# Retention queries decayed by VectorE before the last attention norm, row scalings on ScalarE, and roots as power steps on GpSimd, in a two-block kernel

## What is computed

```python
# attention, per head
w = p[:, :, 0] - lam * p[:, :, 1]
oa = _rms(w @ v, subln_w) * (1.0 - lambda_init)
# retention, per head and direction (chunks of 128, g = decay of the head)
dmat = where(mask, exp(log_g * max(n - m, 0)), 0)
xi   = exp(log_g * (n + 1));  zeta = exp(log_g * (127 - n))
inner = ((q @ k.T) * dmat) @ v
cross = (q * xi) @ state
state = exp(log_g * 128) * state + (k * zeta).T @ v
orr = _rms(forward + backward)              # mean of squares over 128, no weight
mixed = concat([oa * silu(ga), orr * silu(gr)])
x = x + mixed @ w_out
```

## Time and profile before

| | us |
|---|---|
| median of 3 runs | 814.11 |
| lowest, highest | 814.00, 814.99 |
| span of the profiled execution | 811.6 |
| outside the span, by the median | 2.5 |
| TensorE busy | 805.4 (99%) |
| VectorE busy | 634.0 (78%) |
| ScalarE busy | 339.9 (42%) |
| GpSimd busy | 187.8 (23%) |

### The profile page before, as it was taken

How to read it: one execution, slowest core, us unless ns; L and a number is a source line. 1 busy time by engine, 2 the same in 40 slices (tenths; PEclk the granted TensorE clock), 3 DMA queues, 4 the chain that set the end, 5 groups by cost and what they waited for, 6 DMA issues and landing times.

```text
span 811.6 us, 11794 instructions
## 1 busy us (share of the span) xinstructions
PE 805.4 (99%) x4364; PEld 691.4 (85%) x4364; DVE 634.0 (78%) x1112; ACT 339.9 (42%) x721; POOL 187.8 (23%) x189
## 2 busy tenths in 40 slices
PE   9999999999999999999999999999999999999998
PEld 7788888888888888888888888888889988999986
DVE  5998778768984476885578788978798678599998
ACT  4374465632122254342545544551134222455580
POOL 2222111111121221122324555544260114000000
PEclk9999999999999999999999999999999999999999
DMA  7236644445143322336868677596935634866562
GB/s 241 88 96 233 233 155 156 151 161 182 53 156 114 95 78 78 90 93 130 177 144 163 140 151 161 131 182 135 202 104 183 182 98 135 235 184 183 184 203 78
DMA packets 132862, 120.47 MB, mean 148 GB/s; under 512 B 4749, under 2 KB 100550, under 8 KB 132806
## 3 DMA queue, kind: packets, MB, share of 16 engines
q1 hardware_dynamic: 124326, 102.94, 40.9%
q0 software_dynamic: 8448, 16.78, 12.4%
q10 hardware_dynamic: 32, 0.01, 0.0%
HBM read 117.62 MB, written 35.65 MB: 189 GB/s over the span
## 4 chain that ended last, share of the span: by engine, by line
PE 92%; DVE 5%; issue 1%; ACT 1%; DMA 1%; POOL 0%; DVEq 0%; ACTq 0%
PE proj L1886 23%; PE proj L1888 23%; PE proj L1887 23%; PE bank_t L1900 3%; PE bank_o L1975 2%; DVE x L1592 1%; PE score L1888 1%; PE score L1887 1%; PE score L1886 1%; DVE w_lo L1247 1%; PE score L2050 1%; PE score L1960 1%; PE score L1961 1%; PE score L2049 1%; PE bank_o L2068 1%
## 5 line engine op out<-in xcount | busy, mean ns | idle before, releaser
L1247 DVE TENSOR_TENSOR w_lo<-w_raw,w_hi 128x1024 fp32r<-128x1024 f32 x151 | 192.0, 1274 | 44.3 <-POOL w_hi L778 36.1
L778 POOL TENSOR_SCALAR w_hi<-w_raw 128x1024 fp32r<-128x1024 f32 x101 | 118.6, 1174 | 438.6 <-DMA w_raw<-in_w_in_dram 314.6
L1886 PE MATMUL proj<-xt_hi,w_hi 128*128 128x512 f32 (+1 forms) x448 | 171.2, 382 | 0.0
L1888 PE MATMUL proj<-xt_hi,w_lo 128*128 128x512 f32 (+1 forms) x448 | 168.1, 375 | 0.0
L1887 PE MATMUL proj<-xt_lo,w_hi 128*128 128x512 f32 (+1 forms) x448 | 167.8, 374 | 0.0
L1888 PEld LDWEIGHTS proj<-xt_hi,w_lo 128*128 128x128 f32 x448 | 84.4, 188 | 15.6
L1887 PEld LDWEIGHTS proj<-xt_lo,w_hi 128*128 128x128 f32 x448 | 84.5, 189 | 14.1
L1886 PEld LDWEIGHTS proj<-xt_hi,w_hi 128*128 128x128 f32 x448 | 84.5, 189 | 14.0
L1886 PE MATMUL proj<-w_hi,xt_hi 128*128 128x512 f32 x152 | 60.9, 401 | 0.2 <-ACT prob L1012 0.2
L1888 PE MATMUL proj<-w_hi,xt_lo 128*128 128x512 f32 x152 | 59.5, 391 | 0.0
L1887 PE MATMUL proj<-w_lo,xt_hi 128*128 128x512 f32 x152 | 59.4, 391 | 0.0
(11 more groups left out here) (471 smaller groups left out, 1871.2 us busy)
## 6 DMA issues: line engine op xcount, KB each, us to landing
w_raw<-in_w_in_dram SPq DMA_DIRECT2D x79, 512.0 KB, 3.8
w_sums<-in_w_in_dram SPq DMA_DIRECT2D x8, 1024.0 KB, 7.0
w_sums<-w_sums POOLq DMA_DIRECT2D x8, 1024.0 KB, 9.1
w_raw<-w_sums SPq DMA_DIRECT2D x16, 512.0 KB, 3.8
w_raw<-w_sums SPq DMA_DIRECT2D x32, 256.0 KB, 3.3
w_raw<-in_w_out_dram SPq DMA_DIRECT2D x14, 512.0 KB, 3.3
w_raw<-in_w_in_dram SPq DMA_DIRECT2D x26, 256.0 KB, 3.3
w_sums<-in_w_attn_out_dram SPq DMA_DIRECT2D x4, 1024.0 KB, 6.5
```

The costliest lines, as they stand in the source:

```text
L778: pool.tensor_scalar(hi, raw, 1.0, 1.0, ALU.mult, ALU.mult).then_inc(hi_done, 1)
L1247: dve.tensor_tensor(lo, raw, hi.bitcast(F32), ALU.subtract).then_inc(w_split, 1)
L1886: pe.matmul(out, left[0], right[0], start=first, stop=False)
L1888: return pe.matmul(out, left[1], right[0], start=False, stop=last)
```

## The change

- RN 2 and 3 are gone. The plain queries are transposed (RT 2, 3), and VectorE multiplies the transposed queries in PSUM by a table `decays` (rows 0 to 127 of decay along the columns), 4 products of 64x512 for each RT, into `q_decT`. The four transposes of decayed queries are gone: 4 RT steps are left, at g = 17 and 18, ahead of AV, AN and the other steps of their half in every queue.
- `decays` is built by VectorE in DECAYS (g = 2) and DMAT (g = 4, 6, 8, 10), and raised by ScalarE in one Exp over 128x1024 at the end of g = 12.
- ScalarE writes the transposed keys four times, masked to the half of their head (`rk_own`), so that RS uses all 128 rows.
- `rsqrt` of AN 3 writes `rs_o`; ScalarE, not VectorE, scales the rows of attention heads (ON) and of retention heads (RB): 4 copies of 128x128 each, in place.
- RB on VectorE is the sum of squares and one small operation; GpSimd raises the mean to the power -0.5, and ScalarE waits for that.
- KV, RS, RA are one half earlier; F 6 and 7 move from g = 34, 36 to g = 32, 34; RB from g = 25, 27, 31, 33 to g = 24, 26, 28, 30.

```diff
-RET_FIRST = DA_STEPS + 6
-RET_NORMS = (RET_FIRST + 3, RET_FIRST + 5, RET_FIRST + 9, RET_FIRST + 11)
+RET_FIRST = DA_STEPS + 5
+RET_NORMS = (RET_FIRST + 3, RET_FIRST + 5, RET_FIRST + 7, RET_FIRST + 9)
...
+    x = 2 * (g - DA_STEPS - 1)
+    if 0 <= x < 4:
+        out += [("RT", x), ("RT", x + 1)]
     if 3 <= g < DA_STEPS + 3:
         out.append(("AV", g - 3))
...
-    if g == DA_STEPS:
-        out += [("RN", 2), ("RN", 3)]
-    x = 2 * (g - DA_STEPS - 1)
-    if 0 <= x < 8:
-        out += [("RT", x), ("RT", x + 1)]
...
-    finals = {21: 0, 22: 1, 23: 2, 25: 3, 27: 4, 29: 5, 34: 6, 36: 7}
+    finals = {21: 0, 22: 1, 23: 2, 25: 3, 27: 4, 29: 5, 32: 6, 34: 7}
...
+            def retention_root(m):
+                columns = slice(ST * m, ST * m + ST)
+                if m == 0:
+                    pool.memset(minus_half[:], -0.5).then_inc(pool_chain, 1)
+                    pool.wait_ge(pool_chain, 2)
+                pool.wait_ge(o_mean, m + 1)
+                pool.tensor_tensor(rs_o[:, DA_STEPS + ST * m:DA_STEPS + ST * m + ST], ret_mean[:, columns], minus_half[:], ALU.pow).then_inc(o_root, 1)
...
                 act.wait_ge(rt_done, m + 1)
-                if m == 6:
+                if m == 0:
+                    act.wait_ge(halves_set, 4)
+                if m == 2:
                     act.wait_ge(av_done, DA_STEPS)
-                dst = rkT[:, m, :] if m < 2 else q_decT[:, m - 2, :] if m < 6 else rqT[:, m - 6, :]
-                act.activation(dst, score[:, m % 2, :], ACT.Copy).then_inc(rt_free, 1)
+                if m < 2:
+                    for c in range(2):
+                        last = act.activation(rk_own[:, 2 * m + c, :], score[:, m % 2, :], ACT.Copy, scale=half_of[:, c:c + 1])
+                else:
+                    last = act.activation(rqT[:, m - 2, :], score[:, m % 2, :], ACT.Copy)
+                last.then_inc(rt_free, 1)
...
+                        elif kind in ("ON", "RB"):
+                            h = m if kind == "ON" else DA_HEADS + m
+                            act.wait_ge(o_root, 1 if kind == "ON" else m + 2)
+                            for i in range(ST):
+                                o = o_raw[:, h % 4, i, :]
+                                last = act.activation(o, o, ACT.Copy, scale=rs_o[:, ST * h + i:ST * h + i + 1])
+                            last.then_inc(o_normed, 1)
...
                         act.activation(dmat[:], dmat[:], ACT.Exp).then_inc(decay_done, 1)
+                        act.activation(decays[:], decays[:], ACT.Exp).then_inc(decay_done, 1)
...
+                for c in range(2):
+                    dve.tensor_scalar(decays[:, c, h, :], decays[:, c, RET_HEADS - 1, :], log_g[:, 4 * c + h:4 * c + h + 1], None, ALU.mult)
...
+                    elif kind == "RT" and m >= 2:
+                        if m == 2:
+                            dve.wait_ge(decay_done, 3)
+                        dve.wait_ge(rt_free, m + 1)
+                        for c in range(2):
+                            here, h = slice(c * HD, (c + 1) * HD), 2 * (m - 2) + c
+                            for d in range(2):
+                                last = dve.tensor_tensor(q_decT[d * HD:(d + 1) * HD, h, :].rearrange("p (s q) -> p s q", s=ST),
+                                                         score[here, m % 2, :].rearrange("p (s q) -> p s q", s=ST),
+                                                         decays[here, d, h, :].unsqueeze(1).broadcast_to([HD, ST, P]), ALU.mult)
+                        last.then_inc(q_decayed, 1)
...
-                            rsqrt(DA_STEPS, P)
-                    elif kind == "ON":
-                        o = o_raw[:, m, :, :]
-                        dve.tensor_tensor(o, o, rs_y[:, ST * m:ST * m + ST].unsqueeze(2).broadcast_to([P, ST, P]), ALU.mult).then_inc(o_normed, 1)
+                            rsqrt(DA_STEPS, P, rs_o[:, 0:DA_STEPS], o_root)
                     elif kind == "RB":
-                        h = m
-                        head_sums(rs_v[:, 0:ST], sq[:], ST)
+                        mean = ret_mean[:, ST * m:ST * m + ST]
+                        head_sums(mean, sq[:], ST)
                         dve.wait_ge(sq_used, sums[0])
-                        dve.wait_ge(o_normed, DA_HEADS + h)
-                        rsqrt(ST, P)
-                        o = o_raw[:, h, :, :]
-                        dve.tensor_tensor(o, o, rs_y[:, 0:ST].unsqueeze(2).broadcast_to([P, ST, P]), ALU.mult).then_inc(o_normed, 1)
+                        dve.tensor_scalar(mean, mean, 1.0 / P, EPS, ALU.mult, ALU.add).then_inc(o_mean, 1)
...
-                        pe.wait_ge(rt_free, 8)
+                        pe.wait_ge(rt_free, 4)
+                        pe.wait_ge(q_decayed, 1)
+                        pe.wait_ge(ret_scaled, 2)
...
-                    r = slice((m % 2) * HD, (m % 2 + 1) * HD)
+                    else:
+                        pe.wait_ge(q_decayed, 2)
                     for c in range(ST):
-                        last = pe.matmul(score[:, 1, c * P:(c + 1) * P], rkT[r, m // 2, c * P:(c + 1) * P],
-                                         rqT[r, m // 2, c * P:(c + 1) * P], start=True, stop=True)
+                        last = pe.matmul(score[:, 1, c * P:(c + 1) * P], rk_own[:, m, c * P:(c + 1) * P],
+                                         rqT[:, m // 2, c * P:(c + 1) * P], start=True, stop=True)
```

More of the change, by code:

```diff
@@ L346, in build @@
         scoring.close()
-        q_decay = sb("q_decay", [P, ST, RET_HEADS, 2, HD], stack=one)
+        rk_own = sb("rk_own", [P, RET_HEADS, S], stack=one)
         q_decT = sb("q_decT", [P, RET_HEADS, S], stack=one)
@@ L369, in build @@
         diff = sb("diff", [P, TAB], stack=one)
[L370 removed]
         k_decay = sb("k_decay", [P, ST, RET_HEADS, 2, HD], stack=one)
         dmat = sb("dmat", [P, RET_HEADS, P], stack=one)
+        decays = sb("decays", [P, 2, RET_HEADS, P], stack=one)
         lam_s = sb("lam_s", [P, 2], stack=one); lam_e = sb("lam_e", [P, 2], stack=one); neg_lam = sb("neg_lam", [P, 1], stack=one)
@@ L1219, in done, with rsqrt @@
                 dve.wait_ge(dve_chain, chain[0])
-            def rsqrt(n, width):
+            def rsqrt(n, width, out=None, ready=None):
                 v, y, t = rs_v[:, 0:n], rs_y[:, 0:n], rs_t[:, 0:n]
@@ L1226, in rsqrt @@
                 done(dve.tensor_scalar(y.bitcast(I32), t.bitcast(I32), -1.0, float(RSQRT_SEED), ALU.mult, ALU.add))
-                for _ in range(3):
+                for i in range(3):
                     done(dve.scalar_tensor_tensor(out=t, in0=y, scalar=-0.5, in1=y, op0=ALU.mult, op1=ALU.mult))
                     done(dve.tensor_tensor(t, t, v, ALU.mult))
-                    done(dve.scalar_tensor_tensor(out=y, in0=t, scalar=1.5, in1=y, op0=ALU.add, op1=ALU.mult))
+                    if i == 2 and ready is not None:
+                        dve.scalar_tensor_tensor(out=out, in0=t, scalar=1.5, in1=y, op0=ALU.add, op1=ALU.mult).then_inc(ready, 1)
+                    else:
+                        done(dve.scalar_tensor_tensor(out=y, in0=t, scalar=1.5, in1=y, op0=ALU.add, op1=ALU.mult))
             def take_xt_low(m):
@@ L1306, in prepare_decays @@
                 minus_p = diff[:, CENTRE:CENTRE + 1]
-                for k, (sign, steps) in enumerate(((-1.0, 1.0), (1.0, P), (1.0, P - 1.0), (-1.0, 0.0))):
+                for c in range(2):
+                    here, there = halves(c)
+                    dve.memset(half_of[here, c:c + 1], 1.0).then_inc(halves_set, 1)
+                    dve.memset(half_of[there, c:c + 1], 0.0).then_inc(halves_set, 1)
+                for k, (sign, steps) in enumerate(((1.0, P - 1.0), (-1.0, 0.0))):
                     dve.tensor_scalar(steps_to[:, k:k + 1], minus_p, sign, float(steps), ALU.mult, ALU.add).then_inc(dve_chain, 1)
```

40 lines of the change are left out of this document (21 added, 19 removed).

## The result

The changed kernel takes **820.14 us** in the median (819.04 to 822.03), the kernel before 814.69 beside it; the ratio is 1.0063, with a 95% interval of 1.0052 to 1.0074. That is slower, as forecast, but by 5.5 us and not by 2.4, and outside the range. The profiled execution has a span of 817.5 us against 811.6 (+5.9), with 2.6 us outside it by the median.

The account below looks back on a forecast made before the run. TensorE, busy 99%, was taken to set the pace: -3.25 us of its work, +5.2 of waits at F 0 and F 1, +0.5 for a second collision give +2.45 on the span, 816.5 us forecast; range 811.0 to 818.4.

Parts of the forecast that it names:

- After F 1 VectorE has air: Retention heads after F 1: F 2 asked for some 6 us later, 3.1 us a head off VectorE's queue, no stall counted.
- stall up to F 1: TensorE's waits at F 0 and F 1: 5.2 us together, 5.7 with the second collision; F 1 let go at 190.1.
- second collision: GpSimd's rounding of piece 26 at 183.7 meets VectorE's GATE 1 and next split: 0 to 1.0 us, taken as 0.5.
- The mechanism that was forecast: Late VectorE work makes TensorE wait at F 0 and F 1, outweighing its 3.25 us saving; chance 0.62.
- F 0: TensorE asks for it at 181.7, waits 3.35 us until ScalarE has scaled head 0 at 185.05.
- TensorE's saving, -3.25: Work off TensorE: 1.74 us of transposes, 0.76 from RS on 128 rows, 0.75 in what follows RS.
- Start of the products, 172.35: Half g = 18: VectorE starts the products after ScalarE's copy of RT 2, which waits for AV 15.
- The products, 8 x 0.61: Half g = 18: VectorE's eight 64x512 products from PSUM take 4.9 us, until 177.2; bounds 0.35 and 0.76 each.
- First collision, 0.72: GpSimd's rounding of piece 25 at 178.19 stretches VectorE's `rsqrt` by 0.72 us; root ready at 181.2.
- Rival 3: GpSimd's power on the retention means is long, delaying rounding; under 1 us taken, some 832 us at 10; chance 0.05.
- 6 us of room: GpSimd's rounding has some 6 us before KV 3 asks; each microsecond of power beyond costs TensorE one, for four heads.
- DECAYS, DMAT, the larger Exp: Building the decay table early on VectorE and ScalarE: costed at nothing, with 1 us for all other edits in the range.

Follow-up runs that it names:

- e8: The changed kernel with earlier products, GpSimd's power behind the rounding and F 0 to 2 one half later, but RS on 64 rows again: 813.24 us.
- e7: The changed kernel with products ahead of ScalarE's copy, GpSimd's power behind the rounding, and F 0 to 2 one half later: 812.73 us.
- e3: The changed kernel with GpSimd rounding the next piece first and raising the mean to the power after it: 818.03 us.
- e4: The changed kernel with ScalarE scaling attention head 0 ahead of the tanh of gate tile 1: 823.10 us.
- e2: The changed kernel with F 0 put ahead of KV 0 and RS 0 in every queue: 821.23 us.
- e6: The changed kernel with F 0, 1 and 2 at g = 22, 23, 24 instead of 21, 22, 23: 821.76 us.
- e11: e7 with the retention norms' roots taken by VectorE again and no power on GpSimd: 817.73 us.
- e9: The changed kernel with the edits of e3 and e6 together, without the earlier products: 814.50 us.
- e1: The changed kernel with VectorE's products of RT 2 and 3 started before ScalarE's copy of the same bank: 817.63 us.

## Why the prediction came out as it did

The forecast's sum was +2.45 us on the span, and +5.9 came. Two steps of the prediction account for most of the difference of 3.45. "After F 1 VectorE has air" failed: the loop through GpSimd cost 1.6 us at piece 28. And the stall up to F 1 was mis-sized, 6.8 instead of 5.7, by the products (0.70 us instead of 0.61 each) and the second collision (0.84 instead of 0.5). Another 0.4 is in the second block, and some 0.35 has no place. The mechanism that was forecast, waits at F 0 and F 1 that outweigh the saving, took place. Term by term:

- **TensorE's saving, -3.25**: right, as far as rows show it. RS 0.90, RA 1.78, and two RT pairs fewer. What was saved is not what the text names, though ("64 rows to be slower than 128 for equal columns"). The instructions of RS (line 2016) and KV (line 2007) of the kernel before, ns at least, in the median and at most:

```profile
L2016 PE MATMUL score<-rqT,rkT x32: 272/272/373, 185.7 to 214.9; 64*128 64x128 f32 x32
L2007 PE MATMUL score<-vr,k_decay x32: 270/275/275, 184.7 to 213.8; 128*128 128x128 f32 x32
```

  A matmul on 64 rows is as long as one on 128. The extra time stands where TensorE goes from one form to the other: RS starts 0.98 us behind KV and not 0.89, its first matmul takes 0.37 us, and 0.20 falls on the step behind. The rule of the Trainium skill that was weighed against it (TensorEngine Tiling (Array Packing), "Overview") would have made the widening a loss; here nothing runs beside the 64-row matmuls, the rows above gain 0.38 us a head, and e8, with RS on 64 rows, is 0.5 us slower than e7. The measurement decides for 128 rows, in e8 with less than the 1.51 in the sum.
- **Start of the products, 172.35**: right (172.30).
- **The products, 8 x 0.61**: mis-sized. 0.70 each, +0.7. The nearest row was a 128x512 operation of 0.69 us whose follower starts after 0.61; half the rows did not make it shorter, and each product here starts only when the one before it has ended. My bounds held it.
- **First collision, 0.72**: it took place with the rounding that the text names, but cost 0.45, since the rounding had begun 0.46 us ahead of the first step, beside the sum of squares, which it didn't stretch (0.69 us). The root was ready at 181.6 (181.43 and 0.17) against 181.2.
- **F 0**: the wait was 3.93 against 3.35; place and releaser were right. Four scalings took 1.2 us a head (16 in 4.77) against 1.28.
- **Second collision**: mis-sized. The text gave it 0 to 1.0 and took 0.5; the split paid 0.84. With a rounding due at 183.7 and a split at 184.4, both known, the middle of the bounds was no forecast: the operation that starts second waits. The Trainium skill (SBUF — State Buffer, "SBUF: two separate sides") says so, that whoever starts first holds the pair for the whole instruction. By that rule an overlap is paid in full, and the trace agrees in both orders: the split at 2.06 in the changed kernel, the rounding at 1.99 in e3.
- **F 1**: 191.46 against 190.1, to which the text adds 0.5 for the collision. GATE 1 started at 184.20 instead of 183.75 (root and tanh, 0.45), and the collision took 0.84. TensorE, unhindered, would have been there 0.25 earlier than the 184.9 of the text. So the stall was 6.8 instead of 5.7.
- **"After F 1 VectorE has air"**: this step failed, +1.6 us. It counted what leaves VectorE's queue and looked at TensorE's demand for F 2. It did not look at the wait that the change puts into GpSimd's queue: for VectorE's mean, with the rounding queued behind it. Rival 3 had the very order ("waits for VectorE's mean, then raises, then rounds"), but asked only how long the power is. It is 1.02 us; the wait for the mean ahead of it holds the rounding longer (until 202.82 in the first turn, with the piece there at 199.38 in e3). The "6 us of room" ahead of KV 3 was the room of TensorE's demand, not of the loop through both engines, whose turn of 10 us is longer than TensorE's 9.5.
- **The clock**: not in the text. It was free in the changed kernel, and it decided e4 and part of e2, e6 and e11.
- **DECAYS, DMAT, the larger Exp**: at nothing, as said; TensorE's waits up to 170 us are the same as before.
- **The second block**: not in the text. +0.4 us in the changed kernel, 0.3 to 1.0 in its variants. GpSimd, VectorE and TensorE of after, then VectorE of before, in order of time:

```profile
370.31 1.05 POOL L777 TENSOR_SCALAR w_hi<-w_raw 128x1024 fp32r<-128x1024 f32 x1 [5.03 <-DMA w_raw<-in_w_in_dram]
371.39 1.23 DVE L1275 TENSOR_TENSOR w_lo<-w_raw,w_hi 128x1024 fp32r<-128x1024 f32 x1 [0.69 <-POOL w_hi L777]
375.03 0.63 PE L1941 MATMUL bank_t<-ident,stage 128*128 128x128 f32 x4 [0.63 <-DVE yc_hi L1702]
```

```profile
365.47 1.23 DVE L1247 TENSOR_TENSOR w_lo<-w_raw,w_hi 128x1024 fp32r<-128x1024 f32 x1
```

  The split of a piece waits 0.69 us for a rounding that waited for its load, and VectorE's work on the queries, which TensorE waits for, stands behind it; before, that split waits for nothing. Why the load lands later is open, and I made no run for it.

## What to carry to other kernels

Where a change adds a wait to an engine's queue, follow the loop: what stands behind the waiting instruction, who waits for that, and whether this leads back to what the first wait is for. Work out one turn of it and compare it with the pace of the bounding engine; a turn that is 5% longer shows no wait for several turns, and then all of it at once. And a gain in front of such a loop is no gain (e6), until the loop is cut (e9). The busy share of a stretch tells little here: VectorE was busy 18.66 of 20 us in the kernel before and held nobody, and 18.62 in e11, where TensorE waited 3.0 us.

## What the runs showed of the hardware

- After TensorE waited 3.9 us (5.9 in e2, 4.2 in e4, 4.6 in e6, 3.0 in e11) the granted clock was at its lower level, 1.2 GHz, once it worked again: until 3.2 us after F 0 in the changed kernel, 5.6 us after F 1 in e4. Behind e3's 4.1 us TensorE first worked some 1.0 us at 2.4 GHz and fell then (matmuls 0.43 us apart from 187.54 on). Behind e1's 2.3 us it stayed at 2.4 GHz. The price was 0.20 us for each 512-column matmul; in the changed kernel the next wait covered it, in e4 nothing did.
- A product of 64x512 with PSUM as source takes 0.70 us on VectorE, no less than one of 128x512 (0.61 from start to start, or 0.69 busy).
- A matmul on 64 rows takes TensorE as long as one on 128 (272 and 275 ns in the median); changing from one form to the other and back cost 0.38 us a head.
- Where a rounding of GpSimd and a split of VectorE overlap, the one that starts second is stretched: the split to 2.06 us in the changed kernel, the rounding to 1.99 us in e3.
- GpSimd: 128x4 with a power 1.02 us, with a product 0.20 us. In e3, where it ran beside VectorE's work, the same power took 1.88 us.
